# Convolution taps inside the convolution products, and half places at the query/key products, in a one-layer diffusion step

## The reference, cut to what matters

```python
u = ca * jax.nn.sigmoid(cb)                      # ca, cb: slices of h @ w_in
u = (_dwconv_grid(u, w) if latent else _dwconv_seq(u, w)) + b
u = silu(layernorm(u)) @ conv_pw2                # first half of the channels: along a grid row
...                                              # of 64, second half: along a grid column
idx = ...                                        # 8 heads x 16 picks of each token
act = gelu(einsum('td,thkd->thk', xb, u_tab[idx]))
out = einsum('thk,thkd->td', gate * act, v_tab[idx])
```

## Time and profile before

| | us |
|---|---|
| median of 3 runs (lowest, highest) | 3736.16 (3735.05, 3752.05) |
| the profiled execution | 3740.16 |
| its span, first to last instruction | 3738.0 |
| PE busy | 3236.6 (87%) |
| DVE busy | 2709.6 (72%) |
| POOL busy | 1392.1 (37%) |
| ACT busy | 948.0 (25%) |
| the 128 pairs on PE, first to last | 373.2 to 1490.2 |

### The profile page before, as it was taken

How to read it: one execution, slowest core, us unless ns; L and a number is a source line. 1 busy time by engine, 2 the same in 40 slices (tenths; PEclk the granted TensorE clock), 3 DMA queues, 4 the chain that set the end, 5 groups by cost and what they waited for, 6 DMA issues and landing times.

```text
span 3738.0 us, 35693 instructions
## 1 busy us (share of the span) xinstructions
PE 3236.6 (87%) x10985; PEld 1642.8 (44%) x10985; DVE 2709.6 (72%) x6430; ACT 948.0 (25%) x2552; POOL 1392.1 (37%) x1235
## 2 busy tenths in 40 slices
PE   7689899946699987677778699999999999999998
PEld 4355333324344543244434344444444444444444
DVE  2637698776445545888898489788788788776776
ACT  1322322653322112255726401110111101110111
POOL 1001567555454445433233233233333333332331
PEclk9889999967799998888999899999999999999999
DMA  9154888877788898999999999999999999999996
GB/s 363 65 197 132 317 280 305 284 260 286 271 297 293 289 327 318 404 347 368 329 409 383 361 376 400 380 414 401 398 408 416 397 409 406 416 411 405 410 409 273
DMA packets 308332, 1272.13 MB, mean 340 GB/s; under 512 B 30240, under 2 KB 82976, under 8 KB 221872
## 3 DMA queue, kind: packets, MB, share of 16 engines
q0 software_dynamic: 170448, 962.31, 66.6%
q1 hardware_dynamic: 135104, 301.91, 21.8%
q10 hardware_dynamic: 2592, 5.64, 0.4%
HBM read 1220.16 MB, written 49.58 MB: 340 GB/s over the span
## 4 chain that ended last, share of the span: by engine, by line
PE 28%; issue 23%; DVE 20%; DMA 19%; POOL 7%; ACT 4%; SPq 0%; POOLq 0%; DVEq 0%; ACTq 0%
DMA arena<-in_uv,idx 6%; DMA ring_e<-in_uv,idx 6%; PE bank L1153 5%; PE bank L949 5%; PE bank L1123 3%; POOL arena L838 3%; DMA ring_e<-in_v_rows,idx 3%; DVE arena L2000 3%; PE bank L977 3%; DVE ring_e L2000 2%; PE wide L1174 2%; PE wide L892 2%; POOL ring_e L838 2%; DVE arena L2031 2%; PE bank L1241 1%
## 5 line engine op out<-in xcount | busy, mean ns | idle before, releaser
L838 POOL DMA_INDIRECT arena<-in_uv,idx x384 | 445.4, 1160 | 823.6 <-PE bank L1186 511.2
L1241 PE MATMUL bank<-arena 128*128 128x384 f32 x2048 | 693.1, 492 | 60.2 <-ACT arena L1679 37.9
L2000 DVE CUSTOM_DVE_ANT_0 arena<-arena,h2e 128x1024 f32<-128x1024 f32 x384 | 460.7, 1220 | 153.4 <-DMA arena<-in_uv,idx 152.0
L1241 PEld LDWEIGHTS bank<-arena 128*128 128x128 f32 x2048 | 390.4, 192 | 374.7 <-issue 139.4
L838 POOL DMA_INDIRECT ring_e<-in_uv,idx x256 | 304.9, 1191 | 635.6 <-PE bank L1186 361.9
L794 POOL DMA_INDIRECT ring_e<-in_u_rows,idx x256 | 320.4, 1252 | 513.5 <-DVE dots_e L1922 348.5
L1254 PE MATMUL wide<-arena 128*128 128x512 f32 x1024 | 460.9, 593 | 5.1 <-DVE arena L2070 4.8
L1594 ACT ACTIVATE small<-small 128x4 f32<-128x4 f32 x160 | 32.7, 205 | 1425.6 <-DVE small L2000 1425.6
L2000 DVE CUSTOM_DVE_ANT_0 ring_e<-ring_e,h2e 128x1024 f32<-128x1024 f32 x256 | 307.1, 1220 | 99.3 <-DMA ring_e<-in_uv,idx 99.0
L1922 DVE CUSTOM_DVE_ANT_0 ring_e<-ring_e,h2e 128x1024 f32<-128x1024 f32 x256 | 303.4, 1218 | 31.7 <-DMA ring_e<-in_u_rows,idx 31.3
L803 POOL DMA_INDIRECT ring_e<-in_v_rows,idx x256 | 283.7, 1108 | 98.6 <-issue 72.3
(11 more groups left out here) (276 smaller groups left out, 4496.1 us busy)
## 6 DMA issues: line engine op xcount, KB each, us to landing
arena<-in_ut SPq DMA_DIRECT2D x128, 512.0 KB, 7.9
arena<-in_uv SPq DMA_DIRECT2D x128, 512.0 KB, 8.2
arena<-in_w_q SPq DMA_DIRECT2D x48, 512.0 KB, 6.1
spread_d<-arena SPq DMA_DIRECT2D x12, 2048.0 KB, 25.2
arena<-spread_d SPq DMA_DIRECT2D x96, 256.0 KB, 10.7
ring_e<-in_w_mod POOLq DMA_DIRECT2D x16, 1024.0 KB, 9.1
arena<-in_w_cols SPq DMA_DIRECT2D x24, 512.0 KB, 6.5
arena<-in_x SPq DMA_DIRECT2D x20, 512.0 KB, 5.5
```

The source lines that it names most:

```text
L838: pool.indirect_dma_start(out=ring[r], out_offset=None, in_=a["uv"], in_offset=bass.IndirectOffsetOnAxis(ap=idx[kept(t)][:, k:k + 1], axis ...
L1241: ins = pe.matmul(s_bank[:, 0:NC], lhsT=utb[i % URING][:, k * P:(k + 1) * P], rhs=H2T[1][:, k, P:P + NC], start=(k == 0), stop=(k == KD - 1))
L2000: dve.tensor_tensor_reduce(out=ring[r][:, 0:D], in0=ring[r][:, 0:D], in1=h2b[kept(t)], scale=1.0, scalar=0.0, op0=ALU.mult, op1=ALU.add, a ...
```

## The change

Three edits. First, 24 of the 124 latent taps are done earlier, inside the "conv" phase: at six of its eight blocks DVE does four taps between the pair and the wait for the products: four of m = 0 at the third block, four of m = 0 at the fourth, and two of m = 0 and two of m = 1 at each of the last four. The other 100 go, always the m with the fewest done, with 50 sites instead of 41 between them.

Second, "qk" has 18 sites instead of 9: PE calls `early` in the middle of a block too, and is one site further behind than before in this phase. ACT and DVE follow.

Third, the table: "qk" 9 to 12 pairs, "vg" 20 to 23, "gates" 4 to 2, "gla" 24 to 22, "qf1" 17 to 15. The sum stays 128.

```diff
-        for phase, sites, pairs in (("conv", 14, 14), ("qk", 9, 9), ("vg", 32, 20), ("ln", 8, 8), ("gates", 4, 4),
-                                    ("gla", 24, 24), ("out", 16, 16), ("qf0", 16, 16), ("qf1", 16, 17)):
+        for phase, sites, pairs in (("conv", 14, 14), ("qk", 18, 12), ("vg", 32, 23), ("ln", 8, 8), ("gates", 4, 2),
+                                    ("gla", 24, 22), ("out", 16, 16), ("qf0", 16, 16), ("qf1", 16, 15)):
...
-            return pairs_to[max(0, hooks[phase] + n - (phase in ("vg", "qf0", "qf1")))]
+            return pairs_to[max(0, hooks[phase] + n - (phase in ("qk", "vg", "qf0", "qf1")))]
...
-                def project(name, m, b, tb, n):
+                def project(name, m, b, tb, n, site=-1):
...
+                        if k == KD // 2 - 1:
+                            early(s, "qk", site)
...
-                        project("qk", m, *blk)
-                        early(s, "qk", 2 * m + j)
+                        project("qk", m, *blk, site=4 * m + 2 * j)
+                        early(s, "qk", 4 * m + 2 * j + 1)
...
-                early(s, "qk", 8)
+                for i in range(2):
+                    early(s, "qk", 16 + i)
...
                     for j, (b, tb, n) in enumerate(blocks):
+                        early(s, "qk", 4 * m + 2 * j)
                         bk = wait_full(("qk", m, b))
...
+                def tap(m):
+                    j = taps_of[m]
+                    taps_of[m] += 1
...
                 n_ = 0
                 for m in range(CM):
                     for b, tb, n in blocks:
                         early(s, "conv", 2 * n_ - 4)
+                        if s == 1 and n_ >= 2:
+                            for i in range(4):
+                                tap(i % 2 if n_ >= 4 else 0)
                         bk = wait_full(("ca", m, b))
...
-                for j, d in enumerate(offsets):
-                    for m in range(CM):
...
-                        if taps_done * 41 // (TAPS * CM) > (taps_done - 1) * 41 // (TAPS * CM):
-                            early(s, "qk", taps_done * 41 // (TAPS * CM) - 1)
+                left, taps_done = TAPS * CM - sum(taps_of), 0
+                while taps_done < left:
+                    tap(min(range(CM), key=lambda m: (taps_of[m], m)))
+                    taps_done += 1
+                    if taps_done * 50 // left > (taps_done - 1) * 50 // left:
+                        early(s, "qk", taps_done * 50 // left - 1)
```

More of the change, by code:

```diff
@@ L2110, in _ @@
                         pick_step(0, q)
+                offsets = [0] + [d for k in range(1, PAD + 1) for d in (-k, k)]
+                taps_of = [0] * CM
+                def tap(m):
+                    j = taps_of[m]
+                    taps_of[m] += 1
+                    d, w = offsets[j], cw[:, m, offsets[j] + PAD:offsets[j] + PAD + 1]
+                    if j:
+                        dve.wait_ge(*S["tap_done"].at((s, m, j - 1)))
+                    else:
+                        dve.wait_ge(*S["bank_dve"].at(("ca", m, blocks[-1][0])))
+                    if s == 0:
+                        lo, hi = max(0, -d), min(L, L - d)
+                        o, x = C[:, m, lo:hi], U[:, m, lo + d:hi + d]
+                    elif m < CM // 2:
+                        lo, hi = max(0, -d), min(GRID, GRID - d)
+                        g_ = lambda r: r[:, m, 0:L].rearrange("p (r c) -> p r c", c=GRID)
+                        o, x = g_(C)[:, :, lo:hi], g_(U)[:, :, lo + d:hi + d]
+                    else:
+                        lo, hi = max(0, -d) * GRID, min(L, L - d * GRID)
+                        o, x = C[:, m, lo:hi], U[:, m, lo + d * GRID:hi + d * GRID]
+                    if j == 0:
+                        dve.tensor_scalar(o, x, w, cvv[:, 0, m:m + 1], ALU.mult, ALU.add
+                                          ).then_inc(*S["tap_done"].mark((s, m, j)))
+                    else:
+                        dve.scalar_tensor_tensor(out=o, in0=x, scalar=w, in1=o, op0=ALU.mult, op1=ALU.add
+                                                 ).then_inc(*S["tap_done"].mark((s, m, j)))
                 n_ = 0
```

21 lines of the change are left out of this document (removed).

## The result

The changed kernel takes 3755.95 us (median; 3746.28 to 3764.96), the kernel before 3744.07 in the same comparison: ratio **1.0035**, 95% interval 1.0022 to 1.0048. It is some 13 us slower, where I had forecast no change. The time lies inside the range given; what I thought likeliest, no change, is not what came, but a small loss that the measurement can tell from nothing. One of the 14 runs of the kernel before took 6108 us, and the ratio leaves this slow run out.

What follows compares the result with a forecast made beforehand. PE was taken to bound the front, DVE right behind from "qk" on. Terms +20.5 to ln1, -7.6, -2.3, -11.9 and +1 for P48 gave -0.3: 3736 us, no change, chance 0.50, range 3719 to 3758.

Steps and rivals of the forecast that it cites:

- The convolution: 24 taps in "conv": the four at the third block make PE 4.65 us later, later taps are hidden; +4.65 us.
- "qk": Half places in "qk": PE waits about 11 us for P21, until 549.6; stretch with `af` +16.9 us.
- The v and g products: Three more pairs in "vg" at 1.00 us each, half of 12 us of waits kept; L994 at 717, stretch -1.0 us.
- ln: At ln1, P48 is dotted later against L994 than P42 was; +1 us.
- Gates and scans: Two pairs fewer in "gates", two in "gla": -7.6 us up to L2297 and -2.3 us at "gla"'s attend step.
- The -2.3 at the attend step: In "gla", the pair missing at the attend step leaves DVE's path; -2.3 us.
- The tail: Two pairs fewer in "qf1": early sums end 10.8 us earlier behind the last scores; with one block less, -11.9 us reaches the beats.
- (a): Rival: gathers set the pace in "vg" at 7.3 us a pair, L994 at 739, total 3758 us; chance 0.19.
- (b): Rival: each pair leaving "gates", "gla" and "qf1" is worth a gather period of 6.1 us; total 3720 us; chance 0.16.
- (c): Rival: PE finds P19 to P21 in time, "qk" costs only 4.65 us, L994 at 707; total 3725 us; chance 0.15.
- Neither sign: Prediction is wrong if PE does not wait in "qk", or if "vg" runs at over 7 us a pair.

Runs made afterwards that it cites:

- late_pick: Changed kernel with the tile's 29 picking steps spread over 26 pairs instead of 21; ratio 1.0035 to the kernel before, 1.0032 when run again.
- thin_taps: Changed kernel with one tap instead of two at each "qk" site, the 18 taken out moved into the v and g products; ratio 1.0042 to the kernel before.
- gates_alone: Kernel before with "gates" 4 to 2 pairs, "gla" 24 to 22, "vg" 20 to 24; no taps in the convolution, no half places; ratio 1.0035.
- taps_alone: Kernel before with only the 24 taps put inside the convolution, old pairs and sites kept; ratio 0.9999 to the kernel before.

## Why the prediction went wrong, step by step

- **The convolution:** L2155 at the third block stands at 384.50, forecast 384.3. The term was mis-sized, 6.4 and 5.1 us instead of 4.65 (6.9 in the averages over all profiles), because I left out what PE's wait costs behind it: a block of 9.13 us instead of 7.13. PE waits for P1 itself, and not first for P2. The later taps are hidden, as worked out.
- **"qk":** the step is right. PE waits 9.76 us for P21 (forecast 11), and the stretch is +19.4 (forecast +16.9). What holds P21 are mostly the picking steps: moved, they take the wait away (late_pick), while half the taps took 2 us of it (thin_taps). My sum counted both.
- **The v and g products: the failed step.** I wrote that of the 12 us of waits in this stretch half would stay, since fewer taps stand on DVE. They didn't halve: PE needed 149.7 us instead of my 142.5, and 138.5 once the `v` rows were gone. The 12 us were misread too: 8.4 of them are waits in the profile of before, some 3 are products that run slower around waits, and P21's sum, from whose end I counted, ends at 553.2 and not at 552.4. That trace had the reason: POOL's `v` gathers waited 10.1 us for PE between 553 and 697. A further pair here costs 4.8 us (gates_alone), or some 3 with the changed kernel's fewer taps (149.7 us with four pairs more than the 137.9 of taps_alone), not the 1.00 that I summed.
- **ln:** one us for P48 was too little by the same cause; it waited 6.3 us for `v` rows, and the ln stage ended 6.1 us later against ln1 (3.5 in the second profile).
- **Gates and scans:** the step is right where it said most: DVE's offset falls by 7.6 us over the gates in both profiles (38.1 to 30.5, 34.0 to 26.4). The -2.3 at the attend step holds at its place: from the state step before it to the one behind it DVE gains 1.0 to 3.5 us on the kernel before in all ten profiles without that pair, and between a gain of 0.4 and a loss of 2.9 in the six with it. Other steps of the scans lose it again against the one profile of before (+0.5 and -0.9 over all of them).
- **Between the scans and the query products** I had forecast nothing, and the changed kernel loses 5.5 and 6.3 us there against that profile, in which the table is the same. So do nearly all other kernels with this part unchanged (2.9 to 8.1 us, only gates_alone 0.3), so the profile of before seems to be a short one here, which would account for much of what the profiles show over the medians. Why it is short stays open.
- **The tail: failed.** The early sums end 10 us earlier, as worked out, and my sentence that all of it is handed to the beats is false: the scores' way through memory ends 20 to 21 us after their copy, and was as long as the tail before. What failed is the step that took the early sums for the only path to the beats. A second -11.8 us, PE's wait for `w_q` with its slow block, filled the gap in the sum by chance: that is luck; the profile of before showed that wait, and I hadn't asked which transfers it shared the engines with.
- **The rivals:** (a) gave 739 for ln1 and 3758 us in all; the total came near (3756) and ln1 did not (728.65), and its reason is another. (b) is refuted: the two pairs of the gates with the first of the scans were worth 7.6 us, the other of the scans 1.0 to 3.5 at its step, and of the last two one saved 11.8 us by its place and one nothing. (c) too: PE does wait. Neither sign that I had named as showing me wrong came: PE waited in "qk", and "vg" ran at 6.5 us a pair (149.7/23), under my 7.

## What to carry to other kernels

Before a stage gets more work of a kind that runs in a ring, price one more round of that ring, with all that its reuse waits for, and not the work of the engine that is busiest; here 3 to 4.8 us against 1.07. Where a tail is shortened, find the second path that ends at the same place, and how much later it is: two paths of equal length hide each other in a chain of waits. And a wait for a weight load can be ended by leaving a hole in other transfers beside it, where the load itself is issued no earlier.

## What was not expected of the hardware

A load of 512 KB (the median of four) took 22.6 us beside gathers that paused for 4.2 us at most, and 9.0 where these paused for 10.5, at 333 GB/s over the whole stretch in the first case and 318 in the second. And two waits of PE of 5.73 and 9.76 us were each followed by a block of products at 9.13 and 9.03 us instead of 7.13, so the shorter cost about 2 us more than its own length, just as the longer did; in the second profile a wait of 3.32 us did so too (9.03).
